# Sixteen conditioning tiles summed one projection earlier in a hybrid DeltaNet/Conformer encoder

## What is computed

```python
cond = jax.nn.silu(c)
for i in range(DEPTH):
    mod = (cond @ ada_w[i] + ada_b[i])[:, None, :]          # 2048 x 12288 per layer
    sh1, sc1, g1, sh2, sc2, g2 = jnp.split(mod, 6, axis=-1)
    h = rmsnorm(x, norm_w[i, 0]) * (1 + sc1) + sh1
    h = gated_deltanet(...) if i == 0 else conformer_conv(...)
    x = x + (1 + g1) * rmsnorm(h, norm_w[i, 1])
    h = rmsnorm(x, norm_w[i, 2]) * (1 + sc2) + sh2
    h = swiglu(h, ffn_in_w[i], ffn_out_w[i])
    x = x + (1 + g2) * rmsnorm(h, norm_w[i, 3])
```

## Time and profile before

| | |
|---|---|
| median of 3 runs | 3184.55 us (3174.51 to 3184.94) |
| profiled execution | 3177.12 us, its span 3175.5 us |
| TensorE matmul busy | 2926.3 us (92%) |
| VectorE busy | 2248.5 us (71%) |
| ScalarE busy | 1280.5 us (40%) |
| Pool busy | 149.5 us (5%) |
| DMA | 731.61 MB, mean 230 GB/s |
| weight tile and conditioning tile, issue to landing | 5.1 us (input), 8.7 us (output), 6.9 us (conditioning), medians |
| one conditioning sum on VectorE | 2345 ns, 150 of them |

### The profile page before, as it was taken

One profiled execution on the slowest core, in us unless ns is written; L12 is line 12 of the kernel. 1 busy time (PEld: TensorE's weight loads), 2 busy tenths in 40 slices (PEclk: granted clock), 3 DMA queues, 4 the chain that ended last, 5 costly groups with the idle time before them and its releaser, 6 DMA issues.

```text
span 3175.5 us, 37732 instructions
## 1 busy us (share of the span) xinstructions
PE 2926.3 (92%) x13796; PEld 2354.4 (74%) x13796; DVE 2248.5 (71%) x2324; ACT 1280.5 (40%) x1399; POOL 149.5 (5%) x306
## 2 busy tenths in 40 slices
PE   1699999997996997999999999799897999999998
PEld 1577878876885786888888888444675888888886
DVE  6588868987994887878787776368957555555555
ACT  2356644335774334333333332411244333333333
POOL 0011111221111000000000000000000000000000
PEclk8799999999997998999999999999998999999998
DMA  9666766665543996888887877344255665555653
GB/s 375 245 218 230 248 220 225 207 227 162 169 138 121 372 368 243 304 315 336 324 327 296 328 296 275 120 147 149 89 172 189 214 219 199 208 201 203 219 199 119
DMA packets 322174, 731.61 MB, mean 230 GB/s; under 512 B 48128, under 2 KB 64336, under 8 KB 293648
## 3 DMA queue, kind: packets, MB, share of 16 engines
q1 hardware_dynamic: 316256, 709.85, 62.7%
q0 software_dynamic: 5808, 20.35, 1.8%
HBM read 710.45 MB, written 19.69 MB: 230 GB/s over the span
## 4 chain that ended last, share of the span: by engine, by line
PE 83%; DVE 7%; DMA 5%; ACT 3%; issue 2%; SPq 0%; DVEq 0%; POOL 0%; ACTq 0%
PE psg L664 44%; PE psg L670 22%; PE psg L651 5%; DMA aring<-in_ada_w 3%; PE pst L641 1%; DMA wraw<-in_gdn_out_w 1%; PE psn L940 1%; PE psn L691 1%; PE psg L897 1%; DVE wlo L1084 1%; PE psg L869 1%; PE psn L1047 1%; PE pst L856 1%; DVE y L1609 1%; PE psn L641 1%
## 5 line engine op out<-in xcount | busy, mean ns | idle before, releaser
L1733 ACT ACTIVATE whi<-wraw 128x2048 fp32r<-128x2048 f32 x408 | 781.7, 1916 | 1317.5 <-PE psg L670 1163.9
L1084 DVE TENSOR_TENSOR wlo<-wraw,whi 128x2048 fp32r<-128x2048 f32 x408 | 934.8, 2292 | 482.6 <-ACT whi L1733 480.2
L664 PE MATMUL psg<-whi,h_hi 128*128 128x512 f32 x2304 | 731.3, 399 | 33.5 <-DVE h_lo L1689 13.1
L664 PE MATMUL psg<-whi,h_lo 128*128 128x512 f32 x2304 | 720.2, 394 | 0.0
L670 PE MATMUL psg<-wlo,h_hi 128*128 128x512 f32 x2304 | 572.1, 391 | 11.6 <-DVE wlo L1084 11.6
L664 PEld LDWEIGHTS psg<-whi,h_hi 128*128 128x128 f32 x2304 | 435.6, 191 | 127.9 <-issue 25.6
L670 PEld LDWEIGHTS psg<-wlo,h_hi 128*128 128x128 f32 x2304 | 433.5, 188 | 103.7 <-DVE wlo L1084 13.7
L664 PEld LDWEIGHTS psg<-whi,h_lo 128*128 128x128 f32 x2304 | 439.7, 191 | 93.8
L1094 DVE SCALAR_TENSOR_TENSOR aacc<-aring,cond,aacc 128x2048 f32<-128x2048 f32 x150 | 351.8, 2345 | 6.3 <-DMA aring<-in_ada_w 5.8
L651 PE MATMUL psg<-wraw,aring 128*128 128x512 f32 x512 | 221.1, 592 | 0.0
L664 PE MATMUL psg<-whi,g_hi 128*128 128x512 f32 x704 | 219.9, 394 | 0.0
(11 more groups left out here) (251 smaller groups left out, 2517.9 us busy)
## 6 DMA issues: line engine op xcount, KB each, us to landing
aring<-in_ada_w SPq DMA_DIRECT2D x192, 1024.0 KB, 6.9
wraw<-in_ffn_in_w SPq DMA_DIRECT2D x176, 1024.0 KB, 6.8
wraw<-in_gdn_in_w SPq DMA_DIRECT2D x96, 1024.0 KB, 5.1
wraw<-in_ffn_out_w SPq DMA_DIRECT2D x88, 1024.0 KB, 5.2
wraw<-in_cf_pw_w SPq DMA_DIRECT2D x48, 1024.0 KB, 5.5
wraw<-in_gdn_out_w SPq DMA_DIRECT2D x32, 1024.0 KB, 8.7
wraw<-d_rr SPq DMA_DIRECT2D x16, 1024.0 KB, 4.6
x<-in_x SPq DMA_DIRECT2D x2, 2048.0 KB, 8.4
```

The costliest lines, as they stand in the source:

```text
L664: mm(ps[:, t, 0:width], a[:, kc, t * P:(t + 1) * P], wh, start=first and j + n == 0, stop=False)
L1084: tt(wlo[:, j % 2, :], wraw[:, j % 4, :], whi[:, j % 2, :].bitcast(F32), SUB).then_inc(w_lo, 1)
L1733: av(whi[:, j % 2, :], wraw[:, j % 4, :], ACT.Copy).then_inc(w_hi, 1)
```

## The change

FFN shift's 16 tiles get the numbers 48 to 63 in time and are summed in the input projection, so every slice there loads and sums two tiles: the gate's after lo 0 into aacc[0], FFN shift's after lo 2 into aacc[1]. Its fin runs in z after slice 3, its mod_add after lo 18 of z. FFN scale's 16 tiles stay in the output projection, one a tile in slices 1 and 2; slices 0 and 3 have none. Their fin runs after tile 1 of slice 3 and their mod_add after lo of tile 2 there, not after the residual. SP's wait for all of osp_lo moves from behind the load of tile 3 to behind that of tile 7. Pool's two waits become a_used 64 and a_fin 4.

```diff
             def load_qkv(s):
                 for j in range(4):
                     load_w(G_QKV + 4 * s + j, (G_QKV + j) % 4, rows4(gdn_in, j * KT * P, s * NSL))
-                    if j == 2:
-                        load_ada(32 + s, aring, (0, 2), s)
+                    if j % 2 == 0:
+                        load_ada(32 + 2 * s + j // 2, aring, (0, 2 + j // 2), s)
...
             def load_ada2(m):
-                load_ada(48 + m, aring2, (0, 3 + m // KC), m % KC)
+                load_ada(64 + m, aring2, (0, 4), m)
             for j in range(1, 8):
                 load_w(G_GO + j, (G_GO + j) % 4, rows4(gdn_out, j * KT * P, 0))
-                if j == 3:
-                    sp.wait_ge(osp_lo, 8)
-                if j >= 4:
-                    load_ada2(2 * j - 8)
-                    load_ada2(2 * j - 7)
+            sp.wait_ge(osp_lo, 8)
             for n in range(1, 4):
                 for j in range(8):
                     load_w(G_GO + 8 * n + j, (G_GO + j) % 4, rows4(gdn_out, j * KT * P, n * NSL))
-                    load_ada2(8 * n + j)
+                    if n < 3:
+                        load_ada2(8 * n + j - 8)
...
-            fin(48, aacc[:, 0, :])
+            fin(64, aacc[:, 0, :])
             for z in range(2, NZ):
                 z_slice(z, z % 2, first=z == NZ - 1)
+                if z == 3:
+                    pe.wait_ge(mod_ok, 3)
+                    fin(64, aacc[:, 1, :])
...
-                    if n == 1 and j == 7:
-                        fin(64, aacc2)
-            pe.wait_ge(mod_ok, 4)
-            fin(80, aacc2)
+                    if (n, j) == (3, 1):
+                        fin(80, aacc2)
...
-                ada(32 + s, par, aring, aacc[:, 0, :], s, first=start)
+                ada(32 + 2 * s, 0, aring, aacc[:, 0, :], s, first=start)
...
                 lo(g + 2, G_QKV + 2)
+                ada(33 + 2 * s, 1, aring, aacc[:, 1, :], s, first=start)
...
+                if n == 18:
+                    mod_add(4, 3)
...
             for j in range(2, 8):
                 lo(G_GO + j, G_GO + j)
-                if j >= 4:
-                    ada2(2 * j - 8)
-                    ada2(2 * j - 7)
             dve.wait_ge(cw_land, 16)
             for n in range(1, 4):
                 for j in range(8):
                     lo(G_GO + 8 * n + j, G_GO + j)
-                    if n == 2 and j == 0:
-                        mod_add(4, 3)
-                    ada2(8 * n + j)
+                    if (n, j) == (3, 2):
+                        mod_add(5, 4)
+                    if n < 3:
+                        ada2(8 * n + j - 8)
...
             post(0, yg, cwb0)
-            mod_add(5, 4)
             pre(1, y, h_hi3, h_lo3, hf3, 5, 4, lambda: lo(G_F0 + 1, G_F0 + 1))
...
-            pool.wait_ge(a_used, 48)
+            pool.wait_ge(a_used, 64)
...
-            pool.wait_ge(a_fin, 3)
+            pool.wait_ge(a_fin, 4)
```

More of the change, by code:

```diff
@@ L1485, in ada2 @@
             def ada2(m):
-                ada(48 + m, m % 2, aring2, aacc2[:, :], m % KC, first=m % KC == 0)
+                ada(64 + m, m % 2, aring2, aacc2[:, :], m, first=m == 0)
             for j in range(2, 8):
                 lo(G_GO + j, G_GO + j)
-                if j >= 4:
-                    ada2(2 * j - 8)
-                    ada2(2 * j - 7)
             dve.wait_ge(cw_land, 16)
```

## The result

The changed kernel takes 3183.43 us (median of 20 runs, 3175.93 to 3187.78), the kernel before 3176.42 us beside it (20 runs, 3171.10 to 3184.94). The ratio is 1.0023, 95% interval 1.0015 to 1.0031: 7.0 us slower, between 4.8 and 9.8. The forecast was +12.6. Its absolute figure of 3197 missed by 13.6: 5.6 of these are the wrong difference, and 8.1 are the base, since the median of the three runs shown, 3184.55, lies that much above the median of the 20. The measured time lies in the range (3180 to 3211) and in the class forecast (the same, on the slow side); the size of the sum is off.

What follows compares the result with a forecast made beforehand. Input projection taken as bound by TensorE with VectorE close behind, output projection by transfers. Paid 22.0 less 9.4 back gave +12.6, so 3177.1 became 3189.7; with 7 us carried over for the shown median, 3197 us, range 3180 to 3211.

Steps and rivals of the forecast that it cites:

- the order-bound loop: Slices 4 to 9: VectorE's order with ScalarE sets 24.98 us a slice against 24.30; +4.1, bounds 0 and 4.1.
- slices 1 to 3: Input projection: sums ahead of TensorE's wait for VectorE at 208.94 are paid; +5, between 2.3 and 6.8.
- the clock: Kk boundaries: longer waits may turn two more following tiles to the low clock; 0 to 3.2, taken as +1.6.
- the new fin: Z projection after slice 3: fin's 32 small matmuls plus a following tile at the low clock; +5.2 us.
- What gives back: Output projection: 8.6 us of waits for late weights, bounds 7 and 9, plus 0.8 from its fin.
- The fin's part: Output projection: the fin moved to (3,1) costs 5.2 to 6.8 instead of 6.8; −0.8.
- SP's new waits: Output projection: SP waits for tile 64's sum before weight tile 11; costed at nothing, without cover some 3 us a late tile.
- VectorE's slack takes all the sums: Rival for the added sums: 2.4 us idle against 2.27 a slice; 3180 us, chance 0.13.
- Pool first: Rival, slices 4 to 9: kn starts before lo 3, which waits; 1.1 to 2.2 a slice, 3209 us, chance 0.20.
- The kk boundaries: After slices 10 to 13: later conv delays silu, hi and kks, so TensorE waits 1.4 more each; +5.6.
- Into z: Entry of z: VectorE enters some 2.5 us behind, catching up at slice 1's fin; 0 to 2.3, taken as +0.5.

Runs made afterwards that it cites:

- the repeat: The kernel before, profiled once more unedited: 3177.14 us.
- e3: Changed kernel with half a sum more (1024 columns) ahead of the second sum in slices 4 to 15: 3203.77 us, ratio 1.0078 to the kernel before.
- f1: Changed kernel with the second sum of slices 10 to 15 put between lo 1 and conv 0: 3175.39 us, ratio 0.9994 to the kernel before.
- h1: g3 with the second sum of slices 10 to 15 behind conv 3, not ahead of conv 0: 3163.18 us, ratio 0.9960 to the kernel before.
- f2: Changed kernel with both fins after z slice 5, one after the other: 3178.64 us, ratio 0.9998 to the kernel before.
- f4: Changed kernel with slices 10 to 15's second sum before conv 0, both fins after z slice 5, last fin ending the output projection: 3173.08 us.
- g3: f4 with Pool's last product zw started only when VectorE's first exb are done: 3166.27 us, ratio 0.9969 to the kernel before.

## Why the prediction was off, step by step

The forecast of +12.6 us came out at +7.0. The step that failed is the order-bound loop of slices 4 to 9 (4.1 forecast, 0 measured); the term of slices 1 to 3 was over three times too large, those of the clock and of the new fin too small, and what the recurrence gives back was not in the sum at all.

**What gives back.** Right in mechanism. The waits for weights were 8.6 us in the first profile and 8.9 in the repeat (181.20 less 31 steps and the fin's 3.6), and the change takes all of them; 5.5 of the 8.6 are TensorE's idle time, the rest the slower matmuls behind it. Not all of it lies in slice 0, as the forecast had it: 0.6 stand in slice 1 (1095.90). The fin's part is a draw: it cost 6.8 and 3.6 before and 5.2 after, so 10.2 and 7.4 came back for the 9.4 forecast. The cost of nothing at SP's new waits held: TensorE has no wait in the changed output projection.

**Slices 4 to 9: the step that failed.** Forecast 4.1, measured 0. The loop of 24.98 us put silu's table load at 0.1 after lo 0, between conv and silu. Rows 6 had the sign that it isn't there: its idle time ends by Pool's kn, not by the conv. Less its 1.28, the loop is 23.7 and VectorE's work of 24.2 is what binds, under TensorE's 24.4. The upper bound 4.1 was taken as the value, and the lower, 0, was right. The rival "VectorE's slack takes all the sums" was right here and only here, with 0.26 us to spare, as e3 shows: 1.4 us more and a slice is 26.3.

**Pool first.** The rival saw the collision and its deciding point (0.2 us, forecast; 0.38 us, measured). It fell on the good side: lo 3 starts first, kn takes 4.2 us instead of 2.40, and silu's table load waits for it and not TensorE. In e3 the other side came up, at 0.9 us a slice, under the 1.1 to 2.2 forecast.

**Slices 1 to 3.** Forecast 5, measured 1.4, in both pairs of profiles (a wait of 3.76 for 2.38). The step that failed is "VectorE's few waits before it absorb some": they could have been read off. Before 208.94 VectorE idles 1.79 and 0.95 us after the first of the two sums ahead of it, so 4.5 − 2.7 = 1.8 was the value, and the third sum, behind that point, is free. No run tests this alone. VectorE's timeline, the kernel before:

```profile
184.86 0.48 DVE L1306 TENSOR_SCALAR cv<-pst,vec 128x256 f32<-128x256 f32 x1 [1.79 <-PE pst L641]
...
194.99 2.29 DVE L1084 TENSOR_TENSOR wlo<-wraw,whi 128x2048 fp32r<-128x2048 f32 x1 [0.95 <-ACT whi L1733]
```

**The kk boundaries.** Right in mechanism: f1 and h1 take the waits back by moving the sum alone. Waits +5.0 for 5.6. The term of the clock was mis-sized: 4.2 for 1.6. The four first tiles (kks wait to low part) took 3.8, 5.4, 5.4, 3.8 us and now 5.1, 6.6, 5.4, 5.4. Over all 14 profiles: behind waits of 2.64 us 10 of 25 first tiles took 3.8 and 15 took 5.4; behind waits of 3.7 to 4.3 none of 31 took less than 5.1, and one in each of seven profiles took 6.5 or 6.6. So cold tiles went from 15 of 25 to 31 of 31. The sum should have taken its high bound, 3.2, and even that is 1.0 short, for the tile of 6.6. The Trainium skill ("TensorE: Matmul & The Clock Gate", HAM oscillation) says that idle gaps throttle the array again, and by it the term would have been those 3.2; the trace agrees for the longer waits.

**Fins in z.** Forecast 5.2, measured 6.8 in both profiles of the changed kernel. The twin of the earlier trace rows took 3.63 us and only the tile behind it ran cold; within the new fin the granted clock fell (1.00 up to 651, 0.53 behind it), so it took 4.68 and the tile behind it ran cold as well. The 6.8 of the earlier trace rows stood as a second price on the page and was used only as a bound. The price doesn't go with the place: of the 27 single fins with a tile behind them in the 14 profiles one cost 3.6, 19 cost 5.2 and seven 6.8, and the fin of the earlier trace rows cost 6.8 and 3.6 in two profiles of one kernel.

**Into z, rest of z.** 1.2 for 0.5, and 1.6 for a tile behind TensorE's wait for VectorE: not in the sum. It is no draw: behind that wait the step is 5.6 us in all three profiles with the z of the kernel before and 7.2 in all six others that have the wait.

**The recurrence.** A term put at nothing without a word. It gave back 5.6 and 1.8 us in the two pairs, 2.9 on the mean of the seven profiles; without it the sum over them would be +10.4, outside the interval of the runs (4.8 to 9.8). Its spread at the entry is explained by d_rr and zw; whether the mean is an effect of the change stays open.

**Luck.** Forecast 22.0 − 9.4; the first pair of profiles says 20.4 paid, with misses of −3.6, −4.1, +2.0, +0.7, +1.6, +1.6. The paid side was nearly right because they cancel, which is luck; a sum in which slices 4 to 9 cost nothing, slices 1 to 3 the 1.8 of their rows, and the cold tiles and the fin their high bounds would have been nearer in each part.

## What to carry to other kernels

When an operation is added to a nearly full engine, find what its successors wait for, row by row, and place it where that engine already waits: here the second sums of slices 10 to 15 cost 9.2 us at the four boundaries ahead of the convs, and no waiting there behind conv 3, ahead of an idle stretch. A short piece of small matmuls is paid with its own time and often a cold tile; it goes where TensorE waits, or at the end of a stage. Before explaining a few us between two profiles, profile the same kernel twice.

## What the hardware showed that I had not expected

- Pool and VectorE excluded each other for whole instructions, to within 0.2 us: kn 2.40 to 4.17 us behind a lo, a lo 2.28 to 3.16 behind kn; whichever started first (lo by 0.38 us, kn by 1.39) ran at its own time.
- A table load of ScalarE runs ahead of the data wait of its activation: at 333.23, for a silu at 338.24.
- Two fins in a row took 8.72 us in one kernel (f2) and 11.34 to 11.44 in three (f4, g3, h1), where one at full clock takes 3.6: the granted clock falls from 1.00 to 0.50 within them.
- One fin of one unedited kernel cost 6.8 us in one profile and 3.6 in the next.
- One transfer of 1 MB (the first d_rr) took between 16.8 and 20.7 us from issue to landing in 14 profiles.
